# One weight load issued ahead of sixteen small tables, and one ring slot handed back a few instructions sooner

## The reference, cut to what matters

```python
for l in range(2):
    h = rms_norm(x, attn_norm[l])
    proj = h @ w_in[l]            # 1024 x 2472, cut into eleven parts
    ...                           # three mixers: mLSTM, latent attention, spatial gating
    x = x + y @ w_out[l]          # 1024 x 1024
    x = x + hier_moe(rms_norm(x, ffn_norm[l]), ...)
# hier_moe: every token goes to 2 of 32 experts (256 wide):
#   h = silu(xi @ w1[e]) * (xi @ w3[e]);  out += weight * (h @ w2[e])
x = second_block(x, ...)          # 1024 x 6144 projection, two attentions, up and out projections
```

## Time and profile before

| | us |
|---|---|
| three timed runs | 1086.51, 1086.70, 1080.81 |
| their median | 1086.51 |
| the profiled execution, whole | 1084.96 |
| its span, first to last instruction | 1082.7 |
| PE busy in it | 1040.3 (96%) |
| DVE, ACT, POOL busy | 391.2, 283.6, 97.6 |

### The profile page before, as it was taken

How to read it: one execution, slowest core, us unless ns; L and a number is a source line. 1 busy time by engine, 2 the same in 40 slices (tenths; PEclk the granted TensorE clock), 3 DMA queues, 4 the chain that set the end, 5 groups by cost and what they waited for, 6 DMA issues and landing times.

```text
span 1082.7 us, 12843 instructions
## 1 busy us (share of the span) xinstructions
PE 1040.3 (96%) x4537; PEld 536.2 (50%) x4571; DVE 391.2 (36%) x959; ACT 283.6 (26%) x548; POOL 97.6 (9%) x144
## 2 busy tenths in 40 slices
PE   6999999999999998999999999999999999999998
PEld 3586654333333334777554333333334845555443
DVE  1173435433444441542343344443430222333221
ACT  3255332111111113354242111111021006464300
POOL 1320221000000002210220000000000200000000
PEclk9999999999999999999999999999999999999899
DMA  8628238999999996254259999999979248622000
GB/s 288 214 79 311 78 107 300 404 412 412 411 410 413 413 368 229 77 213 177 78 200 343 412 412 411 412 413 412 413 281 391 106 48 288 226 78 78 1 1 39
DMA packets 95325, 280.44 MB, mean 259 GB/s; under 512 B 15957, under 2 KB 29699, under 8 KB 86960
## 3 DMA queue, kind: packets, MB, share of 16 engines
q1 hardware_dynamic: 90208, 273.27, 66.6%
q0 software_dynamic: 5072, 6.56, 1.8%
HBM read 286.99 MB, written 4.72 MB: 269 GB/s over the span
## 4 chain that ended last, share of the span: by engine, by line
PE 74%; SPq 15%; DMA 5%; ACT 3%; issue 2%; DVE 1%; ACTq 0%; DVEq 0%
PE bank L1487 13%; PE bank L930 13%; SPq L592 11%; PE bank L1042 8%; PE bank L962 6%; PE bank L1245 5%; PE bank L881 4%; PE bank L1057 4%; DMA ring<-in_w 3%; PE bank L1617 3%; SPq L598 3%; PE bank L1633 3%; PE bank L1505 3%; PE bank L870 2%; DMA ring<-in_w_in 2%
## 5 line engine op out<-in xcount | busy, mean ns | idle before, releaser
L930 PE MATMUL bank<-ring,arena 128*64 128x512 f32 x1024 | 229.2, 596 | 4.0 <-DMA ring<-in_w 4.0
L1487 PE MATMUL bank<-ring,xfT 128*128 128x512 f32 x320 | 141.5, 596 | 0.0
L930 PEld LDWEIGHTS bank<-ring,arena 128*64 128x64 f32 x1024 | 70.9, 137 | 136.2 <-issue 125.9
L962 PE MATMUL bank<-ring,arena 128*64 128x512 f32 x512 | 116.9, 599 | 0.0
L1042 PE MATMUL bank<-ring,xfT 128*128 128x384 f32 (+2 forms) x256 | 99.6, 542 | 5.1 <-DMA ring<-in_w_in 3.7
L1487 PEld LDWEIGHTS bank<-ring,xfT 128*128 128x128 f32 x320 | 59.3, 190 | 69.2 <-issue 68.3
L881 PE MATMUL bank<-arena 128*128 128x512 bf16 x352 | 86.4, 379 | 1.9 <-issue 0.3
L1655 ACT ACTIVATE arena<-bank 128x512 bf16<-128x512 f32 (+1 forms) x64 | 38.2, 597 | 190.2 <-PE bank L962 190.2
L2002 DVE TENSOR_TENSOR arena<-bank,arena 128x512 f32<-128x512 f32 x60 | 41.5, 692 | 119.3 <-ACT arena L1655 119.3
L1042 PEld LDWEIGHTS bank<-ring,xfT 128*128 128x128 f32 x256 | 49.0, 197 | 45.0 <-issue 25.3
L1648 ACT ACTIVATE arena<-bank,arena 128x256 f32<-128x256 f32 x32 | 15.2, 474 | 201.8 <-PE bank L930 201.8
(11 more groups left out here) (381 smaller groups left out, 1132.9 us busy)
## 6 DMA issues: line engine op xcount, KB each, us to landing
ring<-in_w SPq DMA_DIRECT2D x256, 512.0 KB
ring<-in_w SPq DMA_DIRECT2D x64, 1024.0 KB
ring<-in_w_in SPq DMA_DIRECT2D x14, 2048.0 KB
ring<-in_w_in SPq DMA_DIRECT2D x8, 1536.0 KB
ring<-in_w_out SPq DMA_DIRECT2D x6, 2048.0 KB
x_store<-x POOLq DMA_DIRECT2D x4, 512.0 KB, 6.1
ring<-in_w_up_moba SPq DMA_DIRECT2D x1, 2048.0 KB
ring<-in_w_up_sb SPq DMA_DIRECT2D x1, 2048.0 KB
```

Of the source, the lines that this page charges most:

```text
L930: ins = pe.matmul(bank[5][CELL * e:CELL * (e + 1), :], xg[:, par, 4 * h + k, at:at + CELL], view[:, e, :, k, :], start=(h == 0 and k == 0) ...
L962: ins = pe.matmul(bank[5 + n][CELL * e:CELL * (e + 1), :], turned[:, par, c, CELL * e:CELL * (e + 1)], down_view(s)[:, e, c, n * HALF:(n + ...
L1487: ins = pe.matmul(dst[:, :], xfT[:, k, t * P:(t + 1) * P], w[:, k, :], start=(k == 0), stop=(k == KD - 1))
```

## The change

Two edits. The first moves the place of `mixer_loads` in the first layer: it is now issued behind unit 3's load and ahead of unit 4's, as it already was in the second layer. The second takes the hand-back of slot 4 off the first up matmul of the odd pair and puts it on the first transpose of step 5 in the even pair.

```diff
             for l in range(DEPTH):
                 if mixer:
                     for s in UNIT_ORDER:
-                        if l == 0 and s == UNIT_ORDER[1]:
-                            mixer_loads(l)
-                        if l and s == UNIT_ORDER[2]:
-
-                            sp.wait_ge(x_ready, PER * l)
+                        if s == UNIT_ORDER[2]:
+                            if l:
+                                sp.wait_ge(x_ready, PER * l)
                             mixer_loads(l)
                         c0, c1 = UNIT_COLS[s]
                         if l == 0 and s == UNIT_ORDER[0]:
@@
                                             start=(h == 0 and k == 0), stop=(h == 1 and k == 3))
-                            if par == 1 and h == 0 and k == 0 and e == 0:
-
-                                ins.then_inc(free[DOWN[0]], 1)
                             if h == 1 and k == 0 and e == 0 and free[UP_LO[par]] is not None:
@@
                 if ahead:
                     pe.wait_ge(S["xg_ready"], 2 * q + 3)
-                    gather(1, 1 - par, S, bank[4], free[s] if par == 1 else None)
+                    gather(1, 1 - par, S, bank[4], free[s])
```

## The result

| | before | changed |
|---|---|---|
| timed, median (lowest to highest), us | 1084.10 (1080.52 to 1086.70), 6 runs | 1073.28 (1072.16 to 1076.51), 6 runs |
| ratio, 95% interval | | 0.9908 (0.9881 to 0.9935) |
| profiled execution | 1084.96 | 1074.72 |
| its span | 1082.7 | 1072.4 |
| PE busy | 1040.3 | 1034.0 |

The changed kernel is 0.9% faster, about 10 us, where 6.5 us had been forecast; its 1073.28 lies just under the range. The pause and the slow stretch of the sum's first term went as written, but a new wait took part of that back; the second term was too small; and the profiled pair also differs by a slow stretch of the clock that had been a rival.

What follows compares the result with a forecast made beforehand. PE, busy 96% of the span, was taken as the bound, with loads setting the experts' stage's end. 5.7 + 0.8 = 6.5 us off the 1086.51 median gave 1080.0, range 1074.5 to 1086.0.

Steps and rivals of the forecast that it cites:

- Term one: First mixer's start: the wait for unit 3 (3.72 us) goes and `b2t0` runs at full clock (1.96); 5.7 us saved.
- signs of being wrong: A wait ahead of the tables' transposes or first head unit, 0.50 clock in first mixer, or experts' stage no shorter.
- The tables' cost: First mixer's start: tables behind unit 3 land between 23.8 and 28.2, wanted at 31.4, so they cost nothing.
- The slower rival: First mixer: last table lands at 41.6, wanted at 37.1; 4.5 us more, 0.8 less for slot 4: 1090.2; chance 0.04.
- Term two: Experts' stages: slot 4's earlier hand-back closes DMA holes of 0.4 and 0.7 us; bounds nothing and 1.1, 0.8 taken.
- The bound from the hand-back itself: Experts' stages: SP issues slot 4's load between 1.0 and 1.7 us sooner, 1.3 taken.
- The late slow stretch of the clock: Near 1014 us: the shift may move PE's slow stretch off, 3.1 us more saved: 1076.9; chance 0.12.
- The other rival: First mixer: the wait goes but a half-clock stretch falls elsewhere; 4.5 us saved in all: 1082.0; chance 0.13.
- Unit 3 late: First mixer: unit 3 still late, DMA working on all issued loads at once; only slot 4's gain left: 1085.7; chance 0.05.
- tables late: First mixer: tables take the place of the wait for unit 3 and PE waits longer: 1090.2; chance 0.04.

Runs made afterwards that it cites:

- e5: Kernel before, with five extra matmuls of unit 2, later overwritten, filling PE's wait for unit 3: 1080.11 us against 1081.95, ratio 0.9984.
- e4: Changed kernel with the first layer's tables one place further back, behind unit 4 too: 1073.45 us against 1081.49 for the kernel before.
- e9: Changed kernel with the first layer's tables two places further back, behind units 4 and 5: 1077.40 us against 1082.26 for the kernel before.
- e2: Kernel before with only the earlier hand-back of slot 4, loads in the old order: 1078.26 us against 1081.49, ratio 0.9970.
- e6: Changed kernel with slot 4 handed back still later than in the kernel before: 1082.46 us against 1081.95 for the kernel before.
- e1: Kernel before with only unit 3's load moved ahead of the tables, slot 4 handed back as before: 1076.95 us against 1081.49, ratio 0.9953.
- e8: Changed kernel with slot 0's unit right behind the first layer's tables, slots 2 and 5 handed back sooner: 1072.46 us against 1081.95 for the kernel before.
- e7: The changed kernel again, nothing altered, beside other runs on one chip: 1073.73 us against 1081.95 for the kernel before, ratio 0.9924.

## Why the prediction was right or wrong

**Term one, 5.7 us.** The pause went whole and `b2t0` came back to full clock, as written, with unit 3 there 3.0 us ahead of the latest time computed for it (19.4, not 22.4); e5 shows that the clock's part hangs on the pause. Alone the edit measured 5.1 us by time (3.1 to 7.0), which does not contradict 5.7. The profile shows what the term left out, and it was one of the prediction's own signs of being wrong: "slot 0's unit is the nearest, and I estimate that it just holds because of the idle DMA time that is recovered". It doesn't always hold: most of that time is not recovered, and 1.43 us came back as a new wait in the profiled execution. Without the quicker start, which the change did not make, term one is 3.72 + 1.96 - 1.43 = 4.25 us there. PE asked for slot 0's load 6.5 us sooner than before (at 39.97, not 46.49), and SP issued it only 1.5 us sooner (23.09, not 24.61).

**The tables' cost.** "The same bytes at 386 GB/s throughout take 19.8 us and end at 23.8" was the wrong price. The DMA share falls beside the tables in every order tried (0.42 to 0.91 in steps of 2 us before, 0.46 to 0.91 from 18 to 24 in the changed kernel), and e4 puts their landing near 26.6. The conclusion, that they cost nothing, held, by this estimate with 3.8 us of cover where 3.2 had been given for the worst case. The slower rival, tables that take the place of the wait, is real as a mechanism, but it took one more unit ahead of them to make PE wait at all (0.44 us, e4) and two to make it wait 4.49 us (e9).

**Term two, 0.8 us.** This is the step that failed: "The gain is what the DMA idled for want of that load", with 1.1 us as its upper bound. The stages became 2.0 us shorter in the profiled pair, and e2 measured 3.2 us by time (1.7 to 4.7). I had counted one hole of one or two microseconds per layer, and those holes gave 0.4 us together. The rest came from a second dip that I had not counted: the rate was under 412 GB/s again in the ten microseconds from 22 on, at 388 and 365, and with the earlier slot 4 it is 406 and 413, worth 1.6 us. That "an earlier issue only lengthens the queue" from 200 on was right, but the dip lies before 200. The bound from the hand-back itself, 1.0 to 1.7 us per layer, stood in the same paragraph and was the better one: e6 shows 0.65 to 1 us of stage for each microsecond of hand-back. What the stages don't show of the 3.2 us (the six profiles with the new hand-back and nothing else changed in the stages average 236.0 and 237.1, and the three with the old one 237.5 and 238.2, together 2.6) is 0.6 us and lies inside e2's interval.

**The rivals.** The late slow stretch of the clock was absent in the profiled execution after, which gives 2.6 of its 10.3 us. It was in three profiles (before, e1, e5) and absent in eight. These three are the ones with slot 4's hand-back in its old place, but e6 hands it back later still and had none; no run tells whether this is more than chance. The rival's reason, that a shift in time moves it off, is not borne out: in e2 the same 16 transposes begin at 1013.63, where they begin at 1013.60 before, and run at full clock, and in e1 they begin 5.6 us sooner and are slow. So these 2.6 us of the profiled pair can't be credited to the change, and neither can the quicker start: as far as the runs show, both are luck.

The other rival, that the clock does not come along, rested on the pause of 2.76 us at 408.90 with transposes at full clock behind it. That was one execution too: in e2, e4 and e5 the granted clock falls to 0.50 at the same place (near 412, 405 and 410), and the 16 transposes take 2.9 to 3.6 us. It did not happen at `b2t0` in any profile in which PE had no pause ahead of it.

Of 42 timed runs of the kernel before, in the comparisons of e1 to e8, two had a mean clock of 1.0, and of the changed kernel's twelve, six. In e1's comparison the eight runs of before at 0.995 average 1082.8 us and the two at 1.0 average 1077.7, so most of the spread between runs is the clock. The slow stretch at `b2t0` alone (28.3 to 31.7 at 0.50, of 1083 us) takes the mean clock of a run to 0.998, so in the two runs at 1.0 the pause can't have cost it: the clock's part of term one comes in most executions and not in all. "Unit 3 late" and "tables late" did not happen.

**The forecast as a whole.** It took the change as within 1% of no change, and it is by both comparisons, 0.92% and 0.76%, though the first interval reaches to 1.2%. The 8.2 to 10 us are 1.3 to 1.5 times the 6.5 forecast. In the profiled pair the 3.8 us above the forecast are, within 0.2, 1.2 of term two, 2.6 of the late slow stretch, 1.0 of the quicker start and 0.6 at the turn of the second block, less the 1.4 of slot 0's wait. Of these only term two and slot 0's wait are shown to belong to the change; in e7 the gain was 8.2 us. The stated 1080.0 was 6.7 us too high, and it also leaned on a median of three runs, 1086.51. Three further runs of the same kernel pulled it down to 1084.10, and in the later comparisons it has 1081.49, 1081.95 and 1082.26. The changed kernel kept its 1073 us (1073.28 and 1073.73), so some 2.4 to 5 of the 6.7 us lie in where the forecast began.

## What to carry to other kernels

When a stage is bound by its loads, price an earlier hand-back by how much earlier it is, not by the first hole one sees: here the first holes gave 0.4 us and a dip ten microseconds further on gave 1.6. Look at the rate until it stays level before giving an upper bound. When the order of loads is changed, ask for each consumer when its own load lands (the instruction that waits for it), and do not count a group of small loads at the rate of large ones. A pause on PE may cost once more in the clock behind it; filling it with work that is thrown away tells the two costs apart, if the filler ends when the load lands. Compare several runs and profiles before a stretch of slow clock, a quick start or a median of three is read as an effect of the change.

## What the runs showed of the hardware

Sixteen tables of some 1.5 MB in all went with a DMA rate of 134 to 329 GB/s between 18 and 24 us, although the large loads on both sides moved 370 to 406. Their place in the queue changed when this happened: the lowest rate over 2 us was 117 GB/s at 12 to 14 before, 134 at 18 to 20 in the changed kernel, 149 at 22 to 24 in e4 and 213 at 26 to 28 in e9. Against 386 GB/s it lost 3.6 us before, 2.6 in e2, which has the old order too, and 2.8 in the changed kernel; whether it is less further back, as the higher rate of e9 suggests, one profile of each can't tell. The Trainium skill, "DMA: Bandwidth & Descriptors", section "Measured (HBM→SBUF, 128 partitions, SWDGE, issued from GpSimd)", has transfers under 64 KB as dominated by their descriptors; it was measured there for loads issued from GpSimd, and these are issued from SP. The traces agree in direction (twelve of the sixteen tables are that small) and don't separate it from other causes, such as the gap between SP's issues.

The half clock behind the wait for unit 3 cost different amounts: `b2t0` took 8.83 us behind a pause of 3.72 and 9.67 behind one of 4.35, against 6.87 at full clock. Behind shorter pauses the same instructions ran at either level: with 1.6 to 2.8 us ahead of the second mixer's transposes the granted clock fell to 0.50 in three of the eleven profiles (e2, e4, e5), and with 1.42 us ahead of the 16 transposes near 1014 and 0.99 behind them it fell in three as well (before, e1, e5).
